# Expert rows of a mixture-of-experts layer stored and fetched back by token, instead of combined by matmul

## The reference, cut to what matters

```python
top_vals, top_idx = lax.top_k(logits, TOP_K)          # TOP_K = 2
top_w = jax.nn.softmax(top_vals, axis=-1)
combine = jnp.sum(jax.nn.one_hot(top_idx, N_EXPERTS, dtype=jnp.float32) * top_w[..., None], axis=1)
out = jnp.zeros_like(t)
for e in range(N_EXPERTS):
    y = swiglu(t, w_gate_e[e], w_up_e[e], w_down_e[e])
    out = out + combine[:, e:e + 1] * y
```

## Time and profile before

| | |
|---|---|
| time, median of 3 runs | 1791.04 us (1790.8 to 1792.33) |
| the profiled execution's own time | 1789.35 us |
| its span | 1787.5 us |
| mean granted TensorE clock | 0.995 |
| TensorE busy | 1738.2 us, 97% |
| VectorE busy | 1415.6 us, 79% |
| ScalarE busy | 1175.3 us, 66% |
| read from HBM, written to it | 477.45 MB, 2.10 MB |

### The profile page before, as it was taken

How to read it: one execution, slowest core, us unless ns; L and a number is a source line. 1 busy time by engine, 2 the same in 40 slices (tenths; PEclk the granted TensorE clock), 3 DMA queues, 4 the chain that set the end, 5 groups by cost and what they waited for, 6 DMA issues and landing times.

```text
span 1787.5 us, 23755 instructions
## 1 busy us (share of the span) xinstructions
PE 1738.2 (97%) x8220; PEld 1429.4 (80%) x8220; DVE 1415.6 (79%) x1423; ACT 1175.3 (66%) x1242; POOL 28.5 (2%) x27
## 2 busy tenths in 40 slices
PE   7999999999999999989999999999999999999996
PEld 6777878888887878777888888888888888888885
DVE  7776876544578678769999898898898998988984
ACT  7665765444466667557777777777777777777772
POOL 0200000000002000000000000000000000000000
PEclk9999999999999999989999999999999999999999
DMA  7433345555454333668999999999999999999980
GB/s 284 165 119 126 111 161 184 188 190 182 159 189 165 118 121 120 252 275 338 378 368 340 393 349 369 370 355 373 369 362 374 369 351 384 355 368 379 353 318 25
DMA packets 68408, 480.50 MB, mean 269 GB/s; under 512 B 7920, under 2 KB 8176, under 8 KB 11248
## 3 DMA queue, kind: packets, MB, share of 16 engines
q1 hardware_dynamic: 67328, 475.91, 71.4%
q0 software_dynamic: 1008, 3.67, 0.6%
HBM read 477.45 MB, written 2.10 MB: 268 GB/s over the span
## 4 chain that ended last, share of the span: by engine, by line
PE 77%; DVE 8%; issue 5%; ACT 4%; DVEq 4%; ACTq 1%; DMA 1%; SPq 0%
PE ps_proj L972 9%; PE ps_proj L976 9%; PE ps_proj L975 9%; PE ps_proj L552 7%; PE ps_proj L555 7%; PE ps_proj L554 7%; PE ps_score L972 5%; PE ps_score L976 5%; PE ps_score L975 5%; DVE w_raw_r L2203 3%; PE ps_score L546 2%; PE ps_trans L583 2%; PE ps_ctx L546 2%; PE ps_score L552 1%; PE ps_score L555 1%
## 5 line engine op out<-in xcount | busy, mean ns | idle before, releaser
L2203 DVE TENSOR_TENSOR w_raw_r<-w_raw,hi 128x2048 fp32r<-128x2048 f32 x336 | 759.1, 2290 | 90.6 <-ACT hi L1495 69.6
L1495 ACT ACTIVATE hi<-w_raw 128x2048 fp32r<-128x2048 f32 x335 | 638.9, 1918 | 184.6 <-PE ps_score L976 70.7
L972 PE MATMUL ps_proj<-hi,he_hi 128*128 128x512 f32 x896 | 354.7, 396 | 0.1
L976 PE MATMUL ps_proj<-w_raw_r,he_hi 128*128 128x512 f32 x896 | 349.6, 390 | 0.0
L975 PE MATMUL ps_proj<-hi,he_lo 128*128 128x512 f32 x896 | 349.0, 390 | 0.0
L1116 ACT ACTIVATE hi<-raw 128x2048 fp32r<-128x2048 f32 (+1 forms) x114 | 215.8, 1893 | 124.5 <-PE ps_proj L554 60.6
L1605 DVE TENSOR_TENSOR raw_r<-raw,hi 128x2048 fp32r<-128x2048 f32 (+1 forms) x114 | 257.2, 2265 | 33.3 <-ACT hi L1116 27.1
L552 PE MATMUL ps_proj<-hi,hT_hi 128*128 128x512 f32 (+2 forms) x496 | 197.1, 397 | 6.5 <-DVEq L1591 3.5
L976 PEld LDWEIGHTS ps_proj<-w_raw_r,he_hi 128*128 128x128 f32 x896 | 168.2, 188 | 36.0
L972 PEld LDWEIGHTS ps_proj<-hi,he_hi 128*128 128x128 f32 x896 | 168.3, 188 | 34.8 <-issue 1.5
L975 PEld LDWEIGHTS ps_proj<-hi,he_lo 128*128 128x128 f32 x896 | 168.5, 188 | 33.3
(11 more groups left out here) (347 smaller groups left out, 1996.9 us busy)
## 6 DMA issues: line engine op xcount, KB each, us to landing
w_raw<-in_w_exp SPq DMA_DIRECT2D x336, 1024.0 KB, 6.7
raw<-in_w_pre SPq DMA_DIRECT2D x110, 1024.0 KB, 4.9
raw<-in_w_pre SPq DMA_DIRECT2D x4, 640.0 KB, 6.0
x_tok<-in_x_rows SPq DMA_DIRECT2D x2, 512.0 KB, 5.0
raw<-in_w_pre SPq DMA_DIRECT2D x2, 512.0 KB, 6.0
h_rows<-htok SPq DMA_DIRECT2D x1, 1024.0 KB, 7.9
out_rows<-x_tok SPq DMA_DIRECT2D x1, 1024.0 KB, 4.1
grow<-in_ffn_row SPq DMA_DIRECT2D x1, 512.0 KB, 5.6
```

What stands on the lines that cost most here:

```text
L972: m = nc.tensor.matmul(o, a_hi, w_h, start=first, stop=False)
L976: return nc.tensor.matmul(o, a_hi, w_l, start=False, stop=last)
L1495: A(w_hi[k % HS][:], w_raw[n], ACT.Copy).then_inc(gran_hi, 1)
L2203: V.tensor_tensor(w_low[k % WS], w_raw[k % WS], w_hi[k % HS][:].bitcast(F32), ALU.subtract)\
```

## The change: what it does, and the diff

For the experts 0 to 6 the rows are no longer combined on TensorE. ScalarE writes the weighted rows in float32 (`y_sent`, in `y_hi`'s place), releases the `score` banks itself, and stores the 512 KB to a new HBM tensor `y_rows` with a DMA on its own queue. After the loop VectorE works out for each token in which row of `y_rows` its first and its second expert's result stands (`back_rows`; a row of zeros, stored once by ScalarE, stands for the last expert or an overfull one). GpSimd fetches these rows with four indirect DMAs of 128 rows into `herow` (`fetch_back`), one after another, and VectorE adds each to `x_tok` after the steps 3 to 6 of the last expert (`add_back`). The last expert is still combined by matmuls, now by halves of the width instead of by tokens, its last granule's products are ordered so that `score0` completes first, and the result leaves in four transfers of 256 KB, each after its own add. In both layers' attention two high parts on ScalarE stand later: `hi(at + 14)` after `roots_of(qn0)`, and `hi(at + 16)` after `turned_op(kn0)`.

```diff
@@ sp
-            sp.wait_ge(out_ready, 1)
-            sp.dma_start(out.rearrange("(t p) d -> p t d", p=P), x_tok[:]).then_inc(out_sent, 16)
-            sp.wait_ge(out_sent, 16)
+            for half in range(2):
+                for t in range(TT):
+                    cols = slice(half * 512, (half + 1) * 512)
+                    sp.wait_ge(rows_out[t][half], 1)
+                    sp.dma_start(out[t * P:(t + 1) * P, cols], x_tok[:, t, cols]).then_inc(out_sent, 16)
+            sp.wait_ge(out_sent, TT * 2 * 16)
@@ pe: down
-                        for k in range(2):
+                        order = [(k, b) for k in range(2) for b in range(2)]
+                        if half and c == EXP_CHUNKS - 1:
+                            order = [(k, b) for b in range(2) for k in range(2)]
+                        for k, b in order:
@@ pe: step
-                    if s == EXP_CHUNKS + 1:
-                        pe.wait_ge(y_ready, along(1, rnd, EXPERTS, e, 1))
-                        pe.wait_ge(scatter_ready, along(1, rnd, EXPERTS, e, 1))
-                        combine(0, lambda bank: bank_use(bank, 2, rnd, e))
                     project(1, s, e)
-                    if s == EXP_CHUNKS + 1:
-                        combine(1, lambda bank: bank_use(bank, 3, rnd, e))
-                        scatter_matrix(bank_use("proj2", 3, rnd, e))
@@ pe: last expert
-                pe.wait_ge(y_ready, along(EXPERTS, rnd, EXPERTS))
-                pe.wait_ge(scatter_ready, along(EXPERTS, rnd, EXPERTS))
-                for t in range(TT):
-                    combine(t, lambda bank: bank_use(bank, 1 + t, rnd, last))
+                pe.wait_ge(scatter_ready, along(1, rnd, 1))
+                for half in range(2):
+                    pe.wait_ge(y_ready, along(1 + half, rnd, 2))
+                    for t, bank in enumerate(("ctx", "trans1")):
+                        combine(t, half, bank, bank_use(bank, EXPERTS + half, rnd))
@@ act: attention
                 squares(l, "qn0")
+                roots_of(l, "qn0")
                 hi(at + 14)
-                roots_of(l, "qn0")
                 squares(l, "kn0")
...
                 roots_of(l, "kn1")
+                turned_op(l, "kn0", knT, "kn")
                 hi(at + 16)
-                turned_op(l, "kn0", knT, "kn")
@@ act: outputs
+                    act.wait_ge(y_stored, along(16, rnd, 16 * STORED, e, 16))
+                    y = y_hi if isinstance(e, int) else y_sent
                     for b in range(2):
...
+                        if not isinstance(e, int):
+                            act.drain().then_inc(free[f"score{b}"], 1)
+                    if not isinstance(e, int):
+                        act.wait_ge(y_hi_ready, along(2, rnd, 2 * EXPERTS, e, 2))
...
+                        nc.scalar.dma_start(rows, y_sent[:]).then_inc(y_stored, 16)
@@ act: before the experts
+            act.wait_ge(zeros_set, 1)
+            nc.scalar.dma_start(y_rows[ZERO_ROW:ZERO_ROW + 1, :].rearrange("a (p c) -> p (a c)", p=P), zeros[:])\
+                .then_inc(y_stored, 16)
@@ dve
+            def add_back(n, number):
+                dve.wait_ge(back_in, number(16 * (n + 1)))
+                t = n // 2
+                V.tensor_tensor(x_tok[:, t], x_tok[:, t], herow[:], ALU.add).then_inc(back_added, 1)
+                dve.drain()
...
                     if s == EXP_CHUNKS + 1:
-                        low_outputs(lambda n: along(n, rnd, 2 * EXPERTS, e, 2))
+                        dve.wait_ge(y_hi_ready, along(2, rnd, 2 * EXPERTS, e, 2))
                         weights_on()
...
-                    if s == EXP_CHUNKS + 1:
-                        combined(0, lambda bank: bank_use(bank, 2, rnd, e))
...
-                    if s == EXP_CHUNKS + 1:
-                        combined(1, lambda bank: bank_use(bank, 3, rnd, e))
...
                 last = EXPERTS - 1
+                back_rows()
                 for s in range(2, EXP_CHUNKS):
                     step(s, last, s < EXP_CHUNKS - 1)
+                    if s > 2:
+                        add_back(s - 3, lambda n: along(n, rnd, 2 * TT * 16))
@@ pool
+            def fetch_back(rnd):
+                pool.wait_ge(back_ready, along(1, rnd, 1))
+                pool.wait_ge(he_ready, along(2 * EXPERTS, rnd, 2 * EXPERTS))
+                pool.wait_ge(y_stored, along(16 + 16 * STORED, rnd, 16 * STORED))
+                for n in range(2 * TT):
+                    t, k = n // 2, n % 2
+                    if n:
+                        pool.wait_ge(back_added, along(n, rnd, 2 * TT))
+                    G_.indirect_dma_start(herow[:], None, y_rows,
+                                          bass.IndirectOffsetOnAxis(ap=back_at[:, k, t:t + 1], axis=0))\
+                        .then_inc(back_in, 16)
```

More of the change, by code:

```diff
@@ L244, in build @@
         sc1 = keep("sc1", [8, TT])
+        zeros = keep("zeros", [D // P])
+        back = keep("back", [5, 2, TT])
+        back_at = keep("back_at", [2, TT], U32)
         cnt = keep("cnt", [EXPERTS + 8])
@@ L307, in build @@
         grow = place("grow", [D], base + 32 * K)
+        y_sent = place("y_sent", [D], base + 32 * K)
         y_hi = place("y_hi", [D], base + 32 * K, F32R)
@@ L404, in build @@
         y_ready = sem("y_ready")
-        out_ready = sem("out_ready")
+        rows_out = [[sem(f"rows_out{t}{half}") for half in range(2)] for t in range(TT)]
         out_sent = sem("out_sent")
@@ L959, in scatter_matrix, with combine @@
                 m.then_inc(full["proj2"], 1)
[L961 to L967, removed]
+            def combine(t, half, bank, value):
+                o = take(bank, value)
+                for n, y in enumerate((y_hi, y_lo)):
+                    m = mm(o[:], S[:, t * P:(t + 1) * P], y[:, half * 512:(half + 1) * 512], n, 2)
+                m.then_inc(full[bank], 1)
             def experts(rnd):
@@ L1017, in down @@
                         h, lo_ = granule(k0 + half, e)
-                        for k in range(2):
+                        order = [(k, b) for k in range(2) for b in range(2)]
+                        if half and c == EXP_CHUNKS - 1:
+                            order = [(k, b) for b in range(2) for k in range(2)]
+                        for k, b in order:
                             f = half * 2 + k
[L1020 to L1025, removed]
+                            at_ = slice(k * D + b * 512, k * D + (b + 1) * 512)
+                            m = three(ps[f"score{b}"][:], hidT_hi[:, f], hidT_lo[:, f], h[:, at_], lo_[:, at_],
+                                      c == 0 and f == 0, c == EXP_CHUNKS - 1 and f == 3)
+                            if c == EXP_CHUNKS - 1 and f == 3:
+                                m.then_inc(full[f"score{b}"], 1)
                         if half == 0 or c < EXP_CHUNKS - 1:
@@ L1555, in experts @@
                     step(s, last, s < EXP_CHUNKS - 1)
+                    if s == 3:
+                        scatter_matrix(bank_use("proj2", EXPERTS, rnd))
                 turned(EXP_CHUNKS - 1, last)
-                outputs(lambda bank: bank_use(bank, 0, rnd, last))
+                outputs(last)
             act.preload_act_table_set(exp_ln)
@@ L2279, in experts @@
                 last = EXPERTS - 1
+                back_rows()
                 for s in range(2, EXP_CHUNKS):
                     step(s, last, s < EXP_CHUNKS - 1)
+                    if s > 2:
+                        add_back(s - 3, lambda n: along(n, rnd, 2 * TT * 16))
                 turned(EXP_CHUNKS - 1, last)
                 low_outputs(lambda n: along(n, rnd, 2 * EXPERTS, last, 2))
-                for t in range(TT):
-                    combined(t, lambda bank: bank_use(bank, 1 + t, rnd, last))
+                for half in range(2):
+                    for t, bank in enumerate(("ctx", "trans1")):
+                        o = fresh(bank, bank_use(bank, EXPERTS + half, rnd))
+                        a = x_tok[:, t, half * 512:(half + 1) * 512]
+                        V.tensor_tensor(a, a, o[:], ALU.add).then_inc(rows_out[t][half], 1)
+                        dve.drain().then_inc(free[bank], 1)
                 place8 = slots_of[:, :, 0:EXPERTS]
@@ L2292, in _ @@
             V.memset(eps[:], EPS).then_inc(eps_set, 1)
+            V.memset(zeros[:], 0.0).then_inc(zeros_set, 1)
             for n, s in enumerate(free.values()):
@@ L2306, in _ @@
                     experts(rnd)
-            dve.drain().then_inc(out_ready, 1)
         @block.gpsimd
```

77 lines of the change are left out of this document (54 added, 23 removed).

## The result

| | before | changed |
|---|---|---|
| median, first comparison | 1791.68 us (1790.80 to 1792.85, 4 runs) | 1767.58 us (1767.13 to 1769.73, 4 runs) |
| profiled execution | 1789.35 us, span 1787.5 | 1767.44 us, span 1765.6 |

The ratio is 0.987, 95% interval 0.9855 to 0.9885: the change takes 24.1 us off by the medians and 21.9 us by the two profiled executions. The forecast was 1764.6 us and 26.4 us. One more set of runs on another chip gave 1769.05 us beside 1791.43 (ratio 0.9873, interval 0.9857 to 0.9888).

A forecast was written before the change was run, and what follows sets the result against it. TensorE was taken to bound the expert loop. Terms of -17.5, -4.3, -5.0 and +0.4 sum to -26.4 us: the profiled 1789.35 becomes 1763.0, and with 1.7 for the median the forecast is 1764.6 us, range 1761 to 1770.5.

The forecast's parts named there:

- Bound of the loop: Expert loop: TensorE sets the time, VectorE, ScalarE and DMAs keep up; an expert takes 119.0 us.
- Term 1: Expert loop: combining matmuls of seven experts leave TensorE, 2.5 us each, -17.5 us.
- The rivals on the DMAs: Weight stream: DMAs can't go faster, 1772, chance 0.07; stores among loads lower the rate, 1815 at 350 GB/s, chance 0.03.
- The last expert: Last expert: `back_rows` (3.5 us), fetches and adds fit VectorE's margin; zero, with up to +3 us.
- Term 2: Attention, both layers: two high parts moved later on ScalarE shorten two TensorE pauses, 2 x (1.1 + 1.08) = -4.3 us.
- The second step: Attention: high part moved behind `knT`, which comes 1.8 us sooner; the 1.08 us pause goes in each layer.
- The rival to which I gave 0.10: Attention: pauses only move, VectorE or a later operand holds TensorE instead; term 2 goes, 1769, chance 0.10.
- Term 3: Kernel's end: quarters leave behind their own adds and the adds come 0.8 us sooner, -5.0 us.
- Term 4: Start of the expert stage: DMA issue for the row of zeros ahead of ScalarE's first high parts, +0.4 us.

The follow-up runs named there:

- the run at 410 GB/s: Changed kernel with four further stores of 1 MB each behind the store of each of the seven experts: 1775.30 us, before 1792.03 (0.9904).
- The doubled operations: Changed kernel with the 20 small operations of `back_rows` issued twice, the second result unused: 1774.17 us, before 1791.43 (0.9898).
- the runs with the later rotation: Changed kernel with GpSimd rotating the second tile of `qr` only after VectorE's scaling of `qn0` (1765.05 us), or only after its factors (1765.49 us).

## Why the prediction was nearly right

**Bound of the loop: right.** TensorE kept its pace under VectorE (88.6% busy), ScalarE and the DMAs; the expert takes 119.09 us, 119.0 were forecast.

**Term 1 (-17.5): right, 17.8 measured** once the clock is taken out. Cost of the stores and fetches at nothing: shown by the run without them, to 0.2 us. The rivals on the DMAs fall with the run at 410 GB/s: no product waited for a load. The rule of the Trainium skill that I weighed (HBM binds at about 358 GB/s) doesn't hold for this one core. The skill itself says elsewhere (page "Perfetto Trace Analysis", section "Roofline") that 358 GB/s is the share when both cores of a pair stream, and that a single core can take about 120% of it; the 410 GB/s agree, and that was the sentence to weigh.

**The last expert (zero, up to +3): right.** `back_rows` took 3.6 us (from 1663.01 to 1666.60) where I had 3.5, each addition 1.22 where I had 1.4. `hidT_lo` was ready 0.80 us ahead of TensorE, where 3.53 us of margin less 3.5 of work had left next to nothing. The doubled operations show that this margin decides.

**Term 2 (-4.3): wrong, 0.7 arrives at the router.** The step that failed is "a high part holds ScalarE ..., so the roots start 1.1 us late. Moved behind them it gives back 1.1 of 1.80 us". The roots do come 0.84 us sooner, and nothing follows: VectorE's operations between them and the bank are held by GpSimd's rotation, whose end sets the time. The trace of the kernel before had this: there too the operation that takes 0.17 us by itself took up to 1.17. I had read who ended TensorE's wait and which operation was late, but not the lengths of the small ones between. The run with the first part moved back shows that its move is worth nothing, the runs with the later rotation that GpSimd is the cause. The Trainium skill has the mechanism (page "SBUF — State Buffer", section "SBUF: two separate sides"): VectorE and GpSimd share a port pair under an exclusive lock held for the whole instruction, if VectorE's operation has two SBUF inputs or runs in a two-port mode. The traces agree: each held operation ends with GpSimd's, and the scaling that reads PSUM keeps its 0.69 us beside GpSimd.

The second step, 1.08 us in each layer, was right (1.02 and 1.09 when undone). Against its 2.15 us stand 0.37 and 0.34 us (the pause at 650 us, 1.19 instead of 0.85) behind VectorE's new idle times of 0.48 and 0.49, 0.20 at 589 us, and steps of at most 0.2 us each. What these idle times come from is open: they stand before the same instruction of a program whose other parts changed, and no run here moved them. Up to the router the changed kernel has eight idle times of VectorE over 0.4 us that wait for nothing the profile shows, the kernel before two. What arrives is thus some 1.8 us of the second move less 1.1 that the rest of the change costs. The rival to which I gave 0.10, that the pauses only move, is what half of this term came to, and its 1769 lies nearer to the 1767.6 measured than the 1764.6 of the forecast; the range held because it was drawn to take that rival in.

**Term 3 (-5.0): 4.8 measured.** Behind the last addition 3.9 us are gone (8.9 to 4.95; the run with one transfer gives 4.1), and ahead of it 0.8: from the last full chunk's `down` to the last addition it took 18.97 us and takes 18.14. That the 0.8 is due to the order of the halves is what I had expected; no run changed that order alone.

**Term 4 (+0.4): absent.** The issue stands at 789.14, beside an activation and just ahead of the load of ScalarE's table, where TensorE has only the routing to do; the first matmuls of the stage come as much sooner behind it (0.69 us) as those ahead of it.

**What was not in the sum: the clock, +1.3 in the profile shown.** -17.8 - 0.7 - 4.8 + 1.3 = -22.0, the 21.9 of the two profiled executions. The profile of before that I summed against happened to be one without the fall, 1.7 us under the median then known. The forecast came out 3.0 us too low. Term 2 is 3.6 of that, the small misses of the terms 1, 3 and 4 give 0.5 back, and the fall of the clock was covered by luck: I had added those 1.7 us for the median without asking what they were.

## What to carry to other kernels

When the profile names a late operand, measure every link between it and the engine that is moved, also the small ones: if the same small operation takes 0.17 us in one place and 1.2 in another, look for another engine whose operation ends at the same time; where it holds the chain, work moved on a third gains nothing. A pause of TensorE can cost more than its length: behind the one of 3.6 us the lower clock took another 1.3 to 2.6 us in eleven of twelve profiles. Filling it with products that nobody reads can then pay (2.4 us here), and in the one kernel where this was tried five executions lay within 0.2 us of each other, where the four of the changed kernel beside it spread over 3.0. Before a loop's removed products are counted as time, work out what rate its loads must reach, and look for a stretch of the trace that already reaches it.

## What the runs showed of the hardware

- The granted clock fell behind the pause of 3.4 to 3.7 us in eleven of the twelve profiles that have it (first interval 18.5 to 19.8 us; 17.17 in the one without), and not in the one in which only 0.49 us of the pause were left. Behind a pause of 2.1 to 2.2 us it fell in two profiles of eight, and behind the one of 2.44 us in its only profile.
- VectorE and GpSimd hold each other up: 0.17 became 0.6 to 1.2 us, 0.73 became 2.74, a low part of 2.29 became 3.20, whichever came second waiting for the other's end.
- Four 1 MB stores issued by ScalarE took 2.6 to 3.1 us of its time, 0.7 to 0.8 each, about twice the 0.35 us of the single store of 0.5 MB.
- One core moved 410 GB/s as a mean over 800 us, about a tenth of it stores, with loads landing in 10 us (median).
